# A MoE layer's gated sum moved from the final stage into each expert block: sums gathered from and scattered back to x in DRAM

## What is computed

```python
x = x + merged @ w_o
x = x + HierMoE(RMSNorm(x))      # top-1 of 4 groups, then top-2 of its 8 experts
y = RMSNorm_final(x)

# an expert on its tokens, and the sum over a token's two choices
hid = silu(xb @ w_gate[e]) * (xb @ w_up[e])
moe[token] = sum over its two choices of gate * (hid @ w_down[e])
```

## Time and profile before

| | |
|---|---|
| time, median of 3 runs | 1606.35 us (1604.71 to 1606.37) |
| the profiled execution | 1603.9 us, span of its trace 1602.1 us |
| TensorE busy | 1501.3 us (94%) |
| VectorE busy | 941.3 us (59%) |
| ScalarE busy | 805.6 us (50%) |
| GpSimd busy | 341.6 us (21%) |
| HBM read, written | 300.27 MB, 49.97 MB |

### The profile page before, as it was taken

How to read it: one execution, slowest core, us unless ns; L and a number is a source line. 1 busy time by engine, 2 the same in 40 slices (tenths; PEclk the granted TensorE clock), 3 DMA queues, 4 the chain that set the end, 5 groups by cost and what they waited for, 6 DMA issues and landing times.

```text
span 1602.1 us, 26573 instructions
## 1 busy us (share of the span) xinstructions
PE 1501.3 (94%) x9031; PEld 1322.3 (83%) x9032; DVE 941.3 (59%) x1171; ACT 805.6 (50%) x1058; POOL 341.6 (21%) x396
## 2 busy tenths in 40 slices
PE   5899999999999999998996679999999999999974
PEld 5898998899999899997884568888888888888861
DVE  4425323612334336374666578898986676678956
ACT  4217414702932222452223358877875675578843
POOL 0370073046042000000000112332232222222310
PEclk9999999999999999999997789999999999999997
DMA  6221221232162663563531489999996796699958
GB/s 210 77 64 40 65 80 47 68 97 80 47 213 87 181 121 124 182 222 116 191 101 41 170 322 368 365 382 378 381 386 243 268 370 242 250 364 373 373 229 318
DMA packets 166403, 329.97 MB, mean 206 GB/s; under 512 B 18062, under 2 KB 63416, under 8 KB 165816
## 3 DMA queue, kind: packets, MB, share of 16 engines
q1 hardware_dynamic: 152456, 300.21, 53.6%
q0 software_dynamic: 11568, 20.28, 3.9%
q10 hardware_dynamic: 2304, 8.46, 1.3%
HBM read 300.27 MB, written 49.97 MB: 219 GB/s over the span
## 4 chain that ended last, share of the span: by engine, by line
PE 46%; DVE 3%; DMA 2%; ACT 1%; issue 1%; ACTq 0%; SPq 0%; DVEq 0%; POOLq 0%
PE psum L2208 23%; PE psum L2240 11%; PE psum L2110 6%; PE psum L2191 2%; PE psum L2217 1%; PE psum L2133 1%; DVE expert_lo L2005 1%; DMA expert_raw<-in_w_gate_dram 1%; DMA expert_rows<-block_out,block_out_rows 1%; DMA block_rows<-moe_input,slot_table 0%; PE psum L2179 0%; ACT expert_hi L1796 0%; PE psum L2121 0%; DMA second_rows<-expert_rows 0%; DMA expert_raw<-in_w_down_dram 0%
## 5 line engine op out<-in xcount | busy, mean ns | idle before, releaser
L2005 DVE TENSOR_TENSOR expert_lo<-expert_raw,expert_hi 128x2048 fp32r<-128x2048 f32 x190 | 425.1, 2287 | 84.2 <-ACT expert_hi L1796 84.2
L1796 ACT CAST expert_hi<-expert_raw 128x2048 fp32r<-128x2048 f32 x190 | 350.5, 1903 | 47.9 <-PE psum L2208 18.5
L707 PE MATMUL psum<-w_hi,h_T_hi 128*128 128x256 f32 (+1 forms) x792 | 230.2, 291 | 2.9 <-DVE w_lo L563 2.4
L2208 PE MATMUL psum<-expert_hi,block_T_hi 128*128 128x512 f32 x576 | 229.7, 399 | 1.7 <-DVE block_T_lo L2018 1.5
L2208 PE MATMUL psum<-expert_hi,block_T_lo 128*128 128x512 f32 x576 | 226.4, 393 | 0.0
L2208 PE MATMUL psum<-expert_lo,block_T_hi 128*128 128x512 f32 x576 | 225.9, 392 | 0.0
L707 PE MATMUL psum<-w_hi,h_T_lo 128*128 128x256 f32 (+1 forms) x792 | 223.5, 282 | 0.0
L707 PE MATMUL psum<-w_lo,h_T_hi 128*128 128x256 f32 (+1 forms) x792 | 223.5, 282 | 0.0
L707 PEld LDWEIGHTS psum<-w_hi,h_T_hi 128*128 128x128 f32 (+1 forms) x792 | 141.7, 179 | 10.0 <-issue 6.4
L707 PEld LDWEIGHTS psum<-w_hi,h_T_lo 128*128 128x128 f32 (+1 forms) x792 | 141.7, 179 | 2.6
L707 PEld LDWEIGHTS psum<-w_lo,h_T_hi 128*128 128x128 f32 (+1 forms) x792 | 141.8, 179 | 2.4
(11 more groups left out here) (300 smaller groups left out, 2775.0 us busy)
## 6 DMA issues: line engine op xcount, KB each, us to landing
expert_raw<-in_w_gate_dram SPq DMA_DIRECT2D x64, 1024.0 KB, 9.5
expert_raw<-in_w_up_dram SPq DMA_DIRECT2D x64, 1024.0 KB, 7.6
expert_raw<-in_w_down_dram SPq DMA_DIRECT2D x64, 1024.0 KB, 8.9
w_raw<-in_w_in_dram SPq DMA_DIRECT2D x21, 1024.0 KB, 5.7
gate_logits<-gate_logits_out ACTq DMA_DIRECT2D x16, 516.0 KB, 2.6
gate_logits_even<-gate_logits SPq DMA_DIRECT2D x8, 516.0 KB, 3.7
gate_logits_odd<-gate_logits SPq DMA_DIRECT2D x8, 516.0 KB, 4.3
x_in<-in_x_prompt_dram SPq DMA_DIRECT2D x8, 512.0 KB, 5.1
```

What stands on the lines that cost most here:

```text
L707: m = nc.tensor.matmul(dst, st, mv, start=(k == 0 and n == 0), stop=(k == KD - 1 and n == 2))
L1796: nc.scalar.copy(weh[:, u], wraw[:, SLOT[u]]).then_inc(s_uh[m], 1)
L2005: nc.vector.tensor_tensor(wel[:, u], wraw[:, SLOT[u]], weh[:, u].bitcast(F32), ALU.subtract).then_inc(s_ul[m], 1)
L2208: m = nc.tensor.matmul(bank(m_), x_, w_, start=(u == 0 and k == 0 and i == 0), stop=(u == 1 and k == 3 and i == 2))
```

## The change

- `ys_d` goes. `yb` becomes `ab` (the block's sums), with two index columns and a column of gates `gcol`.
- GpSimd: `gather_sums(b)` waits until the scatter of b-1 has landed, copies two index columns (tokens and assignment numbers), gathers the tokens' rows of `x2_d` into `ab` and each slot's gate from the new array `g_d` into `gcol`. `scatter(b)` writes `ab` back to the same rows of `x2_d`. In the body: gather the rows of b+1, scatter b-2, gather the sums of b-1. Two more clears and a wait for the stored x come ahead of the first block.
- ScalarE: `out_rows` goes; in block 1, after the casts of the down halves, it stores the gates to `g_d` with four DMAs of single elements.
- VectorE: `add_out(b)` adds gate times down product (from PSUM) to `ab`, in two halves of 512 columns. In the body it stands after the low part of the hidden rows and ahead of the splits of the down halves.
- TensorE: the last down product goes to banks 2 and 3 and doesn't wait for `s_y`; the diagonal products of the final stage go.
- Final stage: SP loads only the 9 tiles of `x2_d`, after the last scatter; the earlier loads of x go. ScalarE squares the loaded rows directly; VectorE scales.

Its core:

```diff
-        ys_d = scratch("expert_rows", (2 * TOK, D))
+        g_d = scratch("gate_rows", (2 * TOK, 1))
...
-        yb = r7("block_out", [P, D])
+        ab = r7("block_sums", [P, D])
         idx = r7("block_tokens", [P, 1], I32)
-        odx = r7("block_out_rows", [P, 1], I32)
+        adx = r7("block_sum_rows", [P, 1], I32)
+        gdx = r7("block_gate_rows", [P, 1], I32)
+        gcol = r7("block_gates", [P, 1])
...
-        r8x = Region(r7.at, wraw_at)
-        xf = r8x("x_rows_final", [P, NPRE, D])
-        gfr = r8x("final_norm_row", [P, D])
+        gfr = Region(r7.at, wraw_at)("final_norm_row", [P, D])
...
-        y1 = r8("first_rows", [P, TILES, D])
-        y2 = r8("second_rows", [P, TILES, D])
+        y1 = r8("summed_rows", [P, TILES, D])
+        y2 = r8("normed_rows", [P, TILES, D])
...
-                for t in range(TILES):
-                    if t == NPRE:
-                        sp.wait_ge(s_ul[0], 2 * NE)
-                    sp.dma_start(x_row(t), x2_d[t * P:t * P + rows(t)]).then_inc(s_fx[t], 16)
                 last2 = sp.value_load(nblk[0:1, 1:2], min_val=NE - 2, max_val=NBMAX - 2)
                 sp.wait_ge(s_yo, 16 * last2 + 32)
                 for t in ORDER:
                     r = rows(t)
-                    sp.dma_start(y1[0:r, t, :], ys_d[t * P:t * P + r]).then_inc(s_fi[t], 16)
-                    sp.dma_start(y2[0:r, t, :], ys_d[TOK + t * P:TOK + t * P + r]).then_inc(s_fi[t], 16)
+                    sp.dma_start(y1[0:r, t, :], x2_d[t * P:t * P + r]).then_inc(s_fi[t], 16)
...
                     pool.memset(xg[:, buf], 0.0).then_inc(s_xz, 1)
-                pool.wait_ge(s_xz, 2)
+                pool.memset(ab[:], 0.0).then_inc(s_xz, 1)
+                pool.memset(gcol[:], 0.0).then_inc(s_xz, 1)
+                pool.wait_ge(s_xz, 4)
                 for i in range(2):
                     pool.wait_ge(s_h2o[i], 16 * len(range(i, TILES, 2)))
+                    pool.wait_ge(s_x2o[i], 16 * len(range(i, TILES, 2)))
                 pool.wait_ge(s_tb, 1)
                 count = pool.alloc_register("awaited_count")
...
-                def scatter(b):
+                def gather_sums(b):
                     if later(b, 1):
                         pool.wait_ge(s_yo, 16 * b)
-                    nc.gpsimd.tensor_copy(odx[:], tab[:, bass.ds(b + NBMAX, 1)]).then_inc(s_ox, 1)
+                        pool.wait_ge(s_gs, 16 * b)
+                    nc.gpsimd.tensor_copy(adx[:], tab[:, bass.ds(b, 1)]).then_inc(s_ox, 1)
+                    nc.gpsimd.tensor_copy(gdx[:], tab[:, bass.ds(b + NBMAX, 1)]).then_inc(s_gi, 1)
                     pool.reg_mov(count, b + 1)
                     pool.wait_ge(s_ox, 1)
                     pool.wait_ge(s_ox, count)
+                    pool.wait_ge(s_gi, 1)
+                    pool.wait_ge(s_gi, count)
+                    pool.indirect_dma_start(ab[:], None, x2_d[:, :],
+                                            bass.IndirectOffsetOnAxis(ap=adx[:], axis=0),
+                                            bounds_check=TOK - 1, oob_is_err=False).then_inc(s_ab, 16)
+                    pool.indirect_dma_start(gcol[:], None, g_d[:, :],
+                                            bass.IndirectOffsetOnAxis(ap=gdx[:], axis=0),
+                                            bounds_check=2 * TOK - 1, oob_is_err=False).then_inc(s_gs, 16)
+
+                def scatter(b):
                     pool.reg_mov(count, 2 * b + 2)
-                    pool.wait_ge(s_ox, 1)
+                    pool.wait_ge(s_y, 1)
                     pool.wait_ge(s_y, count)
-                    pool.indirect_dma_start(ys_d[:, :], bass.IndirectOffsetOnAxis(ap=odx[:], axis=0),
-                                            yb[:], None, bounds_check=2 * TOK - 1,
+                    pool.indirect_dma_start(x2_d[:, :], bass.IndirectOffsetOnAxis(ap=adx[:], axis=0),
+                                            ab[:], None, bounds_check=TOK - 1,
                                             oob_is_err=False).then_inc(s_yo, 16)
 
                 def body(b, even, odd):
                     gather(b + 1, 1 - odd)
                     if later(b, 2):
                         scatter(b - 2)
+                    if later(b, 1):
+                        if not later(b, 2):
+                            pool.wait_ge(s_gd, 16 * 4)
+                        gather_sums(b - 1)
                 gather(0, 0)
                 last2 = over_blocks(pool, body)
                 scatter(last2)
+                gather_sums(last2 + 1)
                 scatter(last2 + 1)
+                pool.wait_ge(s_gs, 16 * last2 + 32)
                 pool.wait_ge(s_xg, 16 * last2 + 48)
                 pool.wait_ge(s_yo, 16 * last2 + 32)
 
...
-                def out_rows(b):
-                    act.wait_ge(s_um[2], 2 * b + 2)
-                    if later(b, 1):
-                        act.wait_ge(s_yo, 16 * b)
-                    for half in range(2):
-                        nc.scalar.copy(yb[:, 512 * half:512 * half + 512], bank(5 + half)).then_inc(s_y, 1)
-
...
-                    if later(b, 2):
-                        out_rows(b - 2)
                     if later(b, 1):
                         hidden_hi(b - 1)
                         split_hi(2, b - 1)
+                        if not later(b, 2):
+                            act.wait_ge(s_g2, 1)
+                            with nc.allow_non_contiguous_dma(reason="one gate per token"):
+                                for c in range(2):
+                                    nc.scalar.dma_start(g_d[c * TOK:c * TOK + SEQ].rearrange("(t p) o -> p t o", p=P),
+                                                        gate2[:, 0:NT, c:c + 1]).then_inc(s_gd, 16)
+                                    nc.scalar.dma_start(g_d[c * TOK + SEQ:(c + 1) * TOK],
+                                                        gate2[0:NS, NT, c:c + 1]).then_inc(s_gd, 16)
...
-                out_rows(last2)
-                out_rows(last2 + 1)
-                for n, t in enumerate(BY_PE):
-                    for c in range(2):
-                        nc.scalar.mul(dg[:, n, c, :], ident[:], gate2[:, t, c:c + 1]).then_inc(s_dg, 1)
                 for i, t in enumerate(ORDER):
                     r = rows(t)
-                    if t in BY_PE:
-                        act.wait_ge(s_fp, BY_PE.index(t) + 1)
-                    else:
-                        act.wait_ge(s_f2, BY_DVE.index(t) + 1)
+                    act.wait_ge(s_fi[t], 16)
                     if i:
                         act.wait_ge(s_ms8, i)
-                    nc.scalar.activation(jk8[0:r, :], summed(t), ACT.Square,
+                    nc.scalar.activation(jk8[0:r, :], y1[0:r, t, :], ACT.Square,
...
+                def add_out(b, at=5):
+                    dve.wait_ge(s_um[2], 2 * b + 2)
+                    dve.wait_ge(s_ab, 16 * b + 16)
+                    dve.wait_ge(s_gs, 16 * b + 16)
+                    for half in range(2):
+                        cols = slice(512 * half, 512 * half + 512)
+                        V.scalar_tensor_tensor(ab[:, cols], bank(at + half), gcol[:], ab[:, cols],
+                                               ALU.mult, ALU.add).then_inc(s_y, 1)
...
+                        if later(b, 2):
+                            add_out(b - 2)
...
+                add_out(last2)
+                add_out(last2 + 1, at=2)
                 dve.wait_ge(s_gf, 16)
-                for i in range(TILES + 1):
-                    if i < TILES and ORDER[i] not in BY_PE:
-                        t = ORDER[i]
-                        r, n = rows(t), BY_DVE.index(t)
-                        dve.wait_ge(s_fx[t], 16)
-                        dve.wait_ge(s_fi[t], 32)
-                        nc.vector.scalar_tensor_tensor(y1[0:r, t, :], y1[0:r, t, :], gate2[0:r, t, 0:1],
-                                                       x_row(t), ALU.mult, ALU.add).then_inc(s_f1, 1)
-                        dve.wait_ge(s_f1, n + 1)
-                        nc.vector.scalar_tensor_tensor(y1[0:r, t, :], y2[0:r, t, :], gate2[0:r, t, 1:2],
-                                                       y1[0:r, t, :], ALU.mult, ALU.add).then_inc(s_f2, 1)
-                    if i:
-                        t = ORDER[i - 1]
-                        r = rows(t)
-                        dve.wait_ge(s_sq8, i)
-                        nc.vector.reciprocal(rstd[0:r, t:t + 1], ss[0:r, t:t + 1]).then_inc(s_r8, 1)
-                        dve.wait_ge(s_r8, i)
-                        nc.vector.scalar_tensor_tensor(y2[0:r, t, :], summed(t), rstd[0:r, t:t + 1],
-                                                       gfr[0:r, :], ALU.mult, ALU.mult).then_inc(s_fo, 1)
+                for i, t in enumerate(ORDER):
+                    r = rows(t)
+                    dve.wait_ge(s_sq8, i + 1)
+                    nc.vector.reciprocal(rstd[0:r, t:t + 1], ss[0:r, t:t + 1]).then_inc(s_r8, 1)
+                    dve.wait_ge(s_r8, i + 1)
```

(40 more changed lines are left out.)

15 lines of the change are left out of this document (removed).

## The result

The changed kernel takes 1689.17 us (median; 1688.57 to 1691.53) against 1606.26 us of the kernel before on the same chip: 1.0521 times, 95% interval 1.0503 to 1.0539. Slower, as forecast, but 83 us and not 20, and outside the range. The profiled execution has a span of 1689.4 us, against 1602.1.

What follows compares the result with a forecast made beforehand. TensorE was taken as the bound at 17.68 us a block, VectorE and DMA close behind. The changed loop's round trip adds 29 us, the tail saves 9: 1603.9 + 29 − 9 = 1624 us, range 1593 to 1665.

Steps and rivals of the forecast that it cites:

- That the loop decides: Expert loop: the round trip between two adds takes 19.2 us, 1.5 over TensorE's period; +29 us in all.
- The steps of the round trip: Expert loop, from an add: add, scatter, landing, index copies, sums' and gates' gathers, landing; next add at 19.2 us.
- the landing behind the gates' descriptors: End of the round trip: gates land 3.3 us after their descriptors, as in a light block; 6.2 at full load.
- The scatter's landing: Round trip: 6.6 us from issue to landing, between 3.2 without weights and the median 7.2.
- The count of steps and the cover: Expert loop: 28 steps lose 1.5 us each; 2.7 us of cover before TensorE needs splits counts five times, 13 us.
- The rival "stays loaded": Expert loop: the round trip stays loaded, period 21.5 us, +84 us less 9, 1690 us; chance 0.12.
- The signs: Trace if right: VectorE waits 1 to 2 us for gates per loading block, TensorE for splits; final stage 23 to 28.
- The rival of DMA: Long run of loading blocks: DMA becomes the bound, 5 us lost after 8 of some 14 blocks; 1602 us, chance 0.12.
- VectorE: Expert loop: its two added sums take 1.3 us per block against 1.8 us of rest, fitting with 0.5 to spare.
- The gate stores, priced at nothing: Block 1, ScalarE's queue: four issues where ScalarE waits 12.26 us for gate weights and GpSimd is a block ahead; nothing.
- The gates' elements, priced at nothing in the loop: DMA in the expert loop: 128 gate elements of 4 bytes cost nothing; the ends are nothing and 0.6 us a block.
- The tail: After the loop: last adds and round trips +5.4 us, final stage −14 (25 us for 39.2); together −9, ends −4 and −13.

Runs made afterwards that it cites:

- e1: The changed kernel without the round trip: scatters go to an array nobody reads, the sums' gather doesn't wait for them, two buffers; 1611.4 us.
- e2: The changed kernel with each block's gates gathered one block ahead, before the scatter, into a second column; 1651.0 us.
- e3: e2 with the index column of the next sums copied ahead as well; 1634.1 us.
- e10: The changed kernel with a 128x1024 memset on GpSimd between the index copies and the gather of the sums, which waits for it; 1733.1 us.
- e9: e1 with the rows scaled on ScalarE into a buffer and no adds on VectorE, the gathered sums read by nobody; 1609.3 us.
- e5: The kernel before with only the four gate stores put in, in block 1; 1609.2 us.
- e4: The changed kernel without the gather of sums: ScalarE writes gated rows and the scatter adds them in DRAM; 1612.4 us.
- e6: e4 without gate stores and gate gathers, a constant column standing for the gates; 1606.5 us.
- e7: e4 with a scatter that writes and doesn't add; 1595.7 us.

## Why the prediction was right or wrong

- **That the loop decides, and its mechanism: right.** The round trip through one buffer, with the gates' landing as the last link. e1 (away), e2 and e3 (shorter), e10 (longer) move the time as it says.
- **The steps of the round trip.** From an add at 0, predicted and measured (the step at 1104.15, one of the 21 ordinary ones): scatter issued 2.2 and 2.3; landed 8.8 and 9.9; first copy ends with the last split, 10.4 and 10.5; sums issued 11.5 and 11.5; gates' descriptors written 15.8 and 15.3; landed 19.1 and 20.4. Here the scatter's extra us hid behind the copies, held by the split as foreseen. **The mis-sized term is the landing behind the gates' descriptors**: 3.3 us, the gather of rows in a block without weights, measured 5.0 here and 4.6 in the mean of the 29 loading steps (2.0 to 2.4 in the light ones): 29 × 1.3 = 38 us. I argued that VectorE's stall would thin the loads; they were hardly thinned, 0.90 of the engines. **The scatter's landing was mis-sized too**, 6.6 us for a mean of 7.8 in those 29. In 8 steps that is too late for the copies to hide: GpSimd meets one more split, which the prediction did not count, and the gates' descriptors end at 17.7 us instead of the predicted 15.8. In the other 21 they end at 15.5. Together 29 × 0.34 = 10 us.
- **The count of steps and the cover.** 29 loading steps where 28 were counted: 1.5 us more. The four steps beside blocks without weights, 16.6 us in the mean, give back 4.5 us and not 13: 9 more. So 29 + 38 + 10 + 1.5 + 9 = 87, the measured loss within a us. All the errors went the same way: each took the lighter case.
- **The rival "stays loaded"** gave 1690 and I gave it 0.12. Its argument against itself, that the engines would idle a fifth of the time, was wrong: they idle a tenth in the stretch shown, with TensorE waiting. Its loaded scatter was nearest the truth, but its 1690 is luck: a period of 21.5 (no pieces are given for it) against 20.8 measured, 13 us of cover against 4.5, and nothing for the start, where 8.0 us went.
- **The signs.** VectorE waits for the gates as said, but 3.9 us each time and not 1 to 2; TensorE waits for its gathered rows (42.0 us) and hardly for splits; the final stage is 24.9 us as said.
- **The rival of DMA** was right on its own ground: 5 us lost after 8 blocks of the long run of loading blocks. e9, which has its gathers, lost nothing over the first eight steps (0.8 us), then 6.9 us in ten steps, and 5.5 more in a second stretch, at the end, that I had not counted.
- **VectorE**: fits, as said; e1 against e9 shows no cost of its adds beyond the noise.
- **The gate stores, priced at nothing: wrong**, 3.5 us (e5). I looked at GpSimd's wait and at ScalarE's issues, and not at the loads that share the engines in the one place where TensorE waits for loads.
- **The gates' elements, priced at nothing in the loop: nearly right**, 1.8 us in e4 (over e6), nothing in e7.
- **The tail: right**, −7.2 for −9. The final stage gave 14.3 of 14; the two last round trips cost 3.1 more than before instead of 5.4 (16.2 us from the copy's place to the last landing, against 13.1), and between the last mark of the loop and the last two adds there are 20.0 us (1628.3 to 1648.3) instead of 16.1, which I did not foresee: the gates have landed 3.1 us before that add, and VectorE waits there for the down product; why TensorE is late was not tested. So two errors cancel in part. The end of −4 given with the sum does not follow from its terms either, which make −6.
- **The rule for one DMA** (the Trainium skill, "DMA: Bandwidth & Descriptors", Anatomy of one DMA) gives 2.5 us as an estimate; the scatter took 7.8 in the loop (median) and 2.6 to 3.2 in the tail. In this trace it holds with the queues empty and not beside the loads; by it, as an estimate, the loop would have lost nothing.

No version here that computes everything beats the kernel before; the best of them is e4, 1612.4 us. The lowest of the form with gathered sums is e9, 1609.3 us, that of the adding one e6, 1606.5, and both leave out a part of the work. e7, at 1595.7, shows what the shorter final stage is worth when the loop loses nothing.

## What to carry to other kernels

Before a value is carried through DRAM from one pass of a loop to the next, add up the whole ring (write, landing, wake-up, index, read, landing) with the landing times that the loop has now, under load; if the sum is over the period it sets the period, however idle every engine is. An operation that is cheap in its own engine's time can still be dear where it stands: four stores of 8 KB in all, in the one place where loads are late cost 3.5 us. A ring that shares an engine with long instructions grows in steps and not smoothly: 1 us more cost the 8 blocks that already met the split nothing, and the other 21 twice that. Freed time at the end of a kernel (14 us here) is a single gain, while a microsecond in a loop counts 33 times.

## What the hardware did that I had not expected

- A scatter that adds in DRAM takes 0.7 us more of all 16 engines than a plain one (0.5 MB of buffer, some 57 rows in use), though its packets and bytes are the same in the profile; e4 and e7 differ by 16.7 us for it.
- Descriptor writing by GpSimd takes 1.0 us, or the rest of VectorE's running split and then 1.0, so that moving an issue by 1 us cost 2.0 in one kind of step and nothing in another (e10).
- The landing of the same scatter is 2.6 to 3.2 us with the queues empty and 7.8 to 8.6 (medians of the kernel after, e2 and e3) beside loads, longest in the kernel with the shortest round trip.
